# Float32r weight-ring slots at four offsets to a 512-byte line, and the second half of the activations 256 bytes further

## What is computed

```
r, k, v = xr @ w_r, xk @ w_k, xv @ w_v            # 256 x 2048 by 2048 x 2048
y = rwkv7_scan(...)                               # per head, 64 x 64 states
h = layernorm(ALPHA * h + (y_normed * g) @ w_o)
h = layernorm(ALPHA * h + (silu(h @ w_gate) * (h @ w_up)) @ w_down)
k, v, q = h @ kv_w_k, h @ kv_w_v, h @ w_q
h = layernorm(ALPHA * h + attention(q, k, v) @ w_o)
h = layernorm(ALPHA * h + (silu(h @ w_gate) * (h @ w_up)) @ w_down)
```

## Time and profile before

| | us |
|---|---|
| median of three executions | 2487.11 |
| span of the profiled execution, first to last instruction | 2481.7 |
| TensorE busy (matmul) | 2444.9, 99% |
| TensorE weight loads | 2003.2, 81% |
| VectorE busy | 1410.0, 57% |
| ScalarE busy | 1074.4, 43% |
| 16 DMA engines, q1 and q0 | 54.1% and 2.6% |

### The profile page before, as it was taken

How to read it: one execution, slowest core, us unless ns; L and a number is a source line. 1 busy time by engine, 2 the same in 40 slices (tenths; PEclk the granted TensorE clock), 3 DMA queues, 4 the chain that set the end, 5 groups by cost and what they waited for, 6 DMA issues and landing times.

```text
span 2481.7 us, 39434 instructions
## 1 busy us (share of the span) xinstructions
PE 2444.9 (99%) x15550; PEld 2003.2 (81%) x15550; DVE 1410.0 (57%) x1743; ACT 1074.4 (43%) x1347; POOL 126.0 (5%) x166
## 2 busy tenths in 40 slices
PE   8999999999999999999999999999999999999997
PEld 5888788877888888888887788888788888888886
DVE  6688566676744454454446544666745445454445
ACT  4454355444444444443334344453544444443332
POOL 1000235420000000000000000000000000000000
PEclk9999999999999999999999999999999999999999
DMA  7556411255666666665665565445566666666564
GB/s 233 179 195 205 136 42 38 66 208 188 196 192 188 186 193 186 188 188 193 193 195 198 195 193 188 143 167 190 170 187 192 188 186 193 186 194 221 189 194 143
DMA packets 225435, 440.87 MB, mean 178 GB/s; under 512 B 13472, under 2 KB 23744, under 8 KB 224224
## 3 DMA queue, kind: packets, MB, share of 16 engines
q1 hardware_dynamic: 221760, 417.38, 54.1%
q0 software_dynamic: 3552, 21.73, 2.6%
HBM read 436.96 MB, written 2.10 MB: 177 GB/s over the span
## 4 chain that ended last, share of the span: by engine, by line
PE 94%; DVE 3%; ACT 1%; issue 1%; DMA 1%; POOL 0%; DVEq 0%; ACTq 0%; SPq 0%; POOLq 0%
PE ps L595 25%; PE ps L597 25%; PE ps L596 25%; PE ps L892 3%; PE ps L1075 1%; PE ps L775 1%; PE ps L785 1%; PE ps L1103 1%; PE ps L622 1%; PE ps L624 1%; PE ps L623 1%; PE ps L882 1%; PE ps L836 1%; DVE wlo L1684 1%; PE ps L740 1%
## 5 line engine op out<-in xcount | busy, mean ns | idle before, releaser
L1246 ACT CAST whi<-raw 128x1024 fp32r<-128x1024 f32 x735 | 772.5, 1052 | 1145.9 <-PE ps L597 1080.1
L1684 DVE TENSOR_TENSOR wlo<-raw,whi 128x1024 fp32r<-128x1024 f32 x549 | 670.1, 1225 | 622.2 <-ACT whi L1246 620.3
L595 PE MATMUL ps<-whi,ahi 128*128 128x512 f32 x2172 | 851.5, 392 | 2.8 <-DVE wlo L1684 2.8
L597 PE MATMUL ps<-whi,alo 128*128 128x512 f32 x2172 | 845.6, 389 | 0.0
L596 PE MATMUL ps<-wlo,ahi 128*128 128x512 f32 x2172 | 845.1, 389 | 0.0
L595 PEld LDWEIGHTS ps<-whi,ahi 128*128 128x128 f32 x2172 | 407.8, 188 | 87.6 <-DVE wlo L1684 3.6
L597 PEld LDWEIGHTS ps<-whi,alo 128*128 128x128 f32 x2172 | 407.7, 188 | 85.5
L596 PEld LDWEIGHTS ps<-wlo,ahi 128*128 128x128 f32 x2172 | 407.9, 188 | 84.4 <-issue 1.0
L2015 DVE TENSOR_TENSOR wlo<-raw,whi 128x1024 fp32r<-128x1024 f32 x193 | 236.2, 1225 | 249.4 <-ACT whi L1246 247.4
L595 PE MATMUL ps<-whi,hThi 128*128 128x512 f32 x656 | 255.4, 389 | 0.0
L597 PE MATMUL ps<-whi,hTlo 128*128 128x512 f32 x656 | 255.2, 389 | 0.0
(11 more groups left out here) (317 smaller groups left out, 1933.8 us busy)
## 6 DMA issues: line engine op xcount, KB each, us to landing
raw<-w_up SPq DMA_DIRECT2D x176, 512.0 KB, 3.6
raw<-w_down SPq DMA_DIRECT2D x176, 512.0 KB, 4.0
raw<-w_gate SPq DMA_DIRECT2D x170, 512.0 KB, 3.6
raw<-w_k SPq DMA_DIRECT2D x32, 512.0 KB, 3.8
raw<-w_r SPq DMA_DIRECT2D x32, 512.0 KB, 4.4
raw<-w_v SPq DMA_DIRECT2D x32, 512.0 KB, 3.7
raw<-w_o SPq DMA_DIRECT2D x32, 512.0 KB, 4.8
raw<-kv_v SPq DMA_DIRECT2D x32, 512.0 KB, 3.7
```

The lines of the kernel that those rows point to most:

```text
L595: mm(o, hi[:, k, tok], whi[:, s, k2, :], start=(k == 0), stop=False)
L597: last = mm(o, lo[:, k, tok], whi[:, s, k2, :], start=False, stop=(k == kt - 1))
L1246: nc.scalar.copy(whi[:, s], src).then_inc(hi_done, 1)
L1684: V.tensor_tensor(wlo[:, s], src, whi[:, s].bitcast(F32), ALU.subtract).then_inc(split_done, 1)
```

## The change

Only addresses change. No instruction is added, removed or reordered, and no size of an operand changes. The rings `whi` and `wlo` are each one flat tensor that is 128 bytes longer, and slot n is cut from it at n x 4096 bytes plus a skew: 0, 32, 64, 128 bytes in `whi_ring`, 0, 16, 96, 128 bytes in `wlo_ring` (words times four). `alo` lies 256 bytes further behind `ahi`. `pad_ring` shrinks from 176 to 48 words, `pad_act` (64 words) puts `ahi` back onto a multiple of 512, and `pad_big` goes.

```diff
+SKEW_HI = (0, 8, 16, 32)
+SKEW_LO = (0, 4, 24, 32)
+SKEW_ACT = 64
...
-        pad_ring = sb("pad_ring", [P, 176])
+        pad_ring = sb("pad_ring", [P, 48])
         raw = sb("raw", [P, RING, KC, NB])
         with ExitStack() as early:
             rec2 = sb("rec2", [P, 8192], stack=early)
-        whi = sb("whi", [P, RING, KC, NB], F32R)
-        wlo = sb("wlo", [P, RING, KC, NB], F32R)
+        whi_ring = sb("whi_ring", [P, RING * KC * NB + SKEW_HI[-1]], F32R)
+        wlo_ring = sb("wlo_ring", [P, RING * KC * NB + SKEW_LO[-1]], F32R)
+        pad_act = sb("pad_act", [P, 64])
         with ExitStack() as early:
-            a2t = sb("a2t", [P, 8192], stack=early)
+            a2t = sb("a2t", [P, 8192 + SKEW_ACT], stack=early)
         ahi = sb("ahi", [P, KT, T], F32R)
+        pad_alo = sb("pad_alo", [P, SKEW_ACT])
         alo = sb("alo", [P, KT, T], F32R)
...
-        pad_big = sb("pad_big", [P, 32])
...
+        whi = [carve(whi_ring, n * KC * NB + SKEW_HI[n], KC, NB) for n in range(RING)]
+        wlo = [carve(wlo_ring, n * KC * NB + SKEW_LO[n], KC, NB) for n in range(RING)]
...
-        hF = carve(a2t, KT * T, KT, T)
+        hF = carve(a2t, KT * T + SKEW_ACT, KT, T)
...
-                        mm(o, hi[:, k, tok], whi[:, s, k2, :], start=(k == 0), stop=False)
-                        mm(o, hi[:, k, tok], wlo[:, s, k2, :], start=False, stop=False)
-                        last = mm(o, lo[:, k, tok], whi[:, s, k2, :], start=False, stop=(k == kt - 1))
+                        mm(o, hi[:, k, tok], whi[s][:, k2, :], start=(k == 0), stop=False)
+                        mm(o, hi[:, k, tok], wlo[s][:, k2, :], start=False, stop=False)
+                        last = mm(o, lo[:, k, tok], whi[s][:, k2, :], start=False, stop=(k == kt - 1))
```

More of the change, by code:

```diff
@@ L616, in last_job @@
                         s = (ch + (CF if kt == FT else 0)) % RING
-                        wh, wl = (held_hi[ch - per + kept], held_lo[ch - per + kept]) if ch < per - RING else (whi[:, s], wlo[:, s])
+                        wh, wl = (held_hi[ch - per + kept], held_lo[ch - per + kept]) if ch < per - RING else (whi[s], wlo[s])
                         if t == 0:
@@ L1042, in z_chunk @@
                         o, tok, s = ps[:, 2 * b + t, :], slice(t * P, (t + 1) * P), e % RING
-                        mm(o, ahi[:, k, tok], whi[:, s, k2, :], start=(b == 1 and k == 0), stop=False)
-                        mm(o, ahi[:, k, tok], wlo[:, s, k2, :], start=False, stop=False)
-                        last = mm(o, alo[:, k, tok], whi[:, s, k2, :], start=False, stop=(k == KT - 1))
+                        mm(o, ahi[:, k, tok], whi[s][:, k2, :], start=(b == 1 and k == 0), stop=False)
+                        mm(o, ahi[:, k, tok], wlo[s][:, k2, :], start=False, stop=False)
+                        last = mm(o, alo[:, k, tok], whi[s][:, k2, :], start=False, stop=(k == KT - 1))
                 last.then_inc(chunk_used, 1)
@@ L1186, in out_chunk @@
                         o, tok, s = ps[:, 2 * b + t, :], slice(t * P, (t + 1) * P), e % RING
-                        mm(o, ahi[:, k, tok], whi[:, s, k2, :], start=(k == 0), stop=False)
-                        mm(o, ahi[:, k, tok], wlo[:, s, k2, :], start=False, stop=False)
-                        last = mm(o, alo[:, k, tok], whi[:, s, k2, :], start=False, stop=(k == KT - 1))
+                        mm(o, ahi[:, k, tok], whi[s][:, k2, :], start=(k == 0), stop=False)
+                        mm(o, ahi[:, k, tok], wlo[s][:, k2, :], start=False, stop=False)
+                        last = mm(o, alo[:, k, tok], whi[s][:, k2, :], start=False, stop=(k == KT - 1))
                 last.then_inc(chunk_used, 1)
@@ L1245, in split_hi @@
                         act.wait_ge(chunk_used, c + (ch - RING + 1))
-                    nc.scalar.copy(whi[:, s], src).then_inc(hi_done, 1)
+                    nc.scalar.copy(whi[s], src).then_inc(hi_done, 1)
             act.wait_ge(rows_made, 2)
@@ L1525, in norm_affine @@
                 act.wait_ge(chunk_used, c0 + PLAIN - RING + 1)
-                nc.scalar.copy(whi[:, PLAIN], raw[:, PLAIN]).then_inc(hi_done, 1)
+                nc.scalar.copy(whi[PLAIN], raw[:, PLAIN]).then_inc(hi_done, 1)
                 affine(1)
@@ L1536, in held_out @@
                         act.wait_ge(chunk_used, ch - 2 * RING + 1)
-                    nc.scalar.copy(whi[:, s] if late else held_hi[ch - CHUNKS + 2 * RING], raw[:, s]).then_inc(hi_done, 1)
+                    nc.scalar.copy(whi[s] if late else held_hi[ch - CHUNKS + 2 * RING], raw[:, s]).then_inc(hi_done, 1)
             def ffn(layer):
@@ L1683, in split_lo @@
                     src = land[:, LANDED[c + ch]] if isinstance(c, int) and c + ch in LANDED else raw[:, s]
-                    V.tensor_tensor(wlo[:, s], src, whi[:, s].bitcast(F32), ALU.subtract).then_inc(split_done, 1)
+                    V.tensor_tensor(wlo[s], src, whi[s].bitcast(F32), ALU.subtract).then_inc(split_done, 1)
             then(V.memset(xT[:, :, 0:1], 0.0))
@@ L2012, in residual @@
                         e = ch - CHUNKS + 2 * RING
-                        wh, wl = (held_hi[e], held_lo[e]) if 0 <= e < RING else (whi[:, s], wlo[:, s])
+                        wh, wl = (held_hi[e], held_lo[e]) if 0 <= e < RING else (whi[s], wlo[s])
                         dve.wait_ge(hi_done, ch + 1)
```

## The result

The changed kernel takes 2526.14 us (median of four executions, 2524.05 to 2530.14), the kernel before on the same chip 2486.87 (2484.1 to 2488.41). The ratio is 1.016, 95% interval 1.0146 to 1.0174: 39.3 us slower, where 22 us faster was forecast. This is rival A's figure (33 to 39 us), 0.1 us above the top of the range.

A forecast was written before the change was run, and what follows sets the result against it. The prediction took TensorE's matmul stream, 99% busy, as the bound. Its only nonzero term, 22.5 us gained on the step, took the span from 2481.7 to 2459.2 us, so a median of 2464 us, range 2424 to 2526.

The forecast's parts named there:

- rival A: Four slot offsets upset the regular step every 12 matmuls: 33 us slower (2520 us), at most 39 (2526); chance 0.31.
- What bounds the kernel: TensorE is busy 99% of the span and nothing feeds it late; only the matmul stream's own rate counts.
- the count of 9012: 512-column float32r matmuls in the kernel; at 226.7 ns each they fill 2043 us, 82% of the span.
- 9.0 us per nanosecond: Worth of one nanosecond on the step between matmul starts: 9.0 us, 0.36% of the time.
- Instructions, copies, DMA at 0: No instruction changes; ScalarE's copy, VectorE's subtraction and the DMA are covered by idle time: 0 us each.
- The start of an operand matters: Whether operand offsets to a 512-byte line alter TensorE's step; the trace, with one alignment only, could neither confirm nor refute it.
- rows 6: Trace rows behind an interruption: nine uneven steps in 2.08 us, 231 ns each, the shortest 0.22 us.
- I take a gain ... If half of the changed pairs reach it: Half of the changed pairs step 6.7 ns shorter: mean step down 2.5 ns, a gain of 22.5 us.
- the changed pairs: Moving operand against next stationary tile: 3 in 4 of 9012 pairs, about 6760, get new offset differences; bounds -96 to +39 us.
- The lower bound, the plain step of 216: Step of plain float32 matmuls of 256 columns, 10.7 ns below 226.7; reached by every pair it would return 96 us.
- point from which it decides: The slower rival wins once a change of offset upsets the step and no offset wins back over 4 ns.
- Range: Over all cases 2424 us, taking in about half of the large gain, to 2526 us, the slower rival's full price.

The follow-up runs named there:

- offsets_alone: TensorE alone, no kernel: 52 series of 512-column float32r matmuls at set operand offsets; the change's pattern stepped at 231.0 ns, good series settled at 226.7.
- uniform_32: Against the kernel before: all eight slots of both rings at 32 bytes, activations on a 512-byte line; 2541.27 us, ratio 1.0223.
- all_32: Against the kernel before: both rings at 32 bytes and ahi, alo, hThi, hTlo at 32 bytes as well; 2486.78 us against 2485.49, ratio 1.0006.
- offsets_pairs: TensorE alone, no kernel: more matmul series varying offsets, stationary columns and plain float32; moving offsets of 16 to 224 bytes stepped at 231 to 235 ns.
- by_256: The change's form with every skew a multiple of 256 bytes, against the kernel before; 2485.89 us, ratio 1.0003.

## Why the prediction was wrong

- *What bounds the kernel, the count of 9012 and 9.0 us per nanosecond*: right. The loss is in TensorE's stream, and 4.4 ns x 9012 gives the 39.3 us.
- *Instructions, copies, DMA at 0*: right. 1049 and 1224 ns, q1 at 53.5%, the ring waits at 2.4 us. That the other engines do not disturb TensorE's reads is shown by offsets_alone.
- *The start of an operand matters*: right, as rows 6 suggested, and through the pairs of moving and stationary operand as the part on the change set them out. The Trainium skill's page "TensorE: Matmul & The Clock Gate", Part 2, step on LDWEIGHTS, would have had no effect at all here. uniform_32 and all_32 differ only in where the stationary tiles lie against the moving ones, as far as these matmuls go, and by 54 us. So the step that the prediction drew from the page's "doesn't steal", 226.7 ns wherever the operands lie, does not hold, and the measurement decides. Whether the two reads take bandwidth from one another is not shown: shorter weight loads did not shorten the step.
- *"I take a gain ... If half of the changed pairs reach it"*: this is the step that failed. The one term of the sum, the changed pairs, was put at -22.5 us and measured +39.3: the mean step went from 226.7 to 231.0 ns, where 224.2 was forecast. The 0.22 us of rows 6 was one member of an uneven run whose mean was 231, so taking it as a value that a pair could hold was a pick and no bound. It was also misread: the rows give starts to 10 ns, and in the trace's nanoseconds that step is 224, 2.7 ns below 226.7 and not 6.7; no step between matmuls of lines 595 to 597 in the kernel before is shorter. None of the 505 layouts settles below 226.67.
- *The lower bound, the plain step of 216*: reached by none of them either. It is the step of one pass over 256 columns; a pass of plain float32 over 512 columns steps at 429 ns (offsets_pairs). The prediction set it beside the page's 215.8 ns for 512 columns; that the two agree is no test of the page's figure at 512 columns.
- *Rival A* had the size (33 to 39 us for 231 ns; measured 39.3) but not the reason. It blamed the change of offset every 12 matmuls. Slots that differ by 256 bytes cost nothing (by_256), slots that are all alike at 32 bytes cost most (uniform_32). Its "point from which it decides" was wrong. That its number came out is luck: the mean over many layouts, 231.9, happens to lie close to the 231 of the uneven run in rows 6.
- *Range*: its top, 2526, was rival A's full price with nothing beyond it. That bound came from the mean of one uneven run, while single differences hold 233.3 ns (uniform_32, +54.8 us), which the trace of the kernel before could not show.

## What to carry to other kernels

Where TensorE's float32r matmuls follow one another without a gap, look at the start-to-start step and at the offsets of both operands modulo 256 bytes: keep the moving and the stationary operand at the same one, a multiple of 32 bytes. That was worth 12.9 us here where only the down projections had it wrong, and 54.8 where all were 32 bytes apart; which multiple of 32 it is made no difference in the series and kernels above, and a pad ahead of one tensor can shift everything behind it out of step. When a quantity in the trace is uneven, price a disturbance by its mean, not by its best member, and don't take a difference of 7 ns from starts that are given to 10.

## What the runs showed of the hardware that was not expected

- The step of 512-column float32r matmuls tends to settle on a ladder of 6.67 ns per cycle of a pattern: 226.67, 228.89, 231.11, 233.33 ns for patterns of three (314 of 505 series), and 246.67 for the two slowest. Why the ladder exists, and where the 10.7 ns over the plain step come from, no run settles; fewer stationary columns did not lower the step below 226.7.
- One layout can hold two steps: a difference of 64 bytes stepped at 229.2 and 233.4 ns in two runs of TensorE alone; the kernel with it came out at the lower one (+18.1 us).
- A plain float32 matmul is two passes: 40 of them left 80 records and took 34.50 us, 0.86 us each (last rows of offsets_pairs). The 216 ns that the prediction used as its yardstick are the step of one pass over 256 columns.
- At 256 columns the order turns round. The series of 90 float32r matmuls at equal offsets starts 10.79 us before the next, at 32 bytes of difference, and that one 10.61 before the third, at 128: 119.9 and 117.9 ns a step.

```profile
701.45 10.96 PE L232 MATMUL ps<-mov,sta 128*128 128x256 f32 x90
712.24 10.77 PE L225 MATMUL ps<-mov,sta 128*128 128x256 f32 x90
722.85 10.83 PE L232 MATMUL ps<-mov,sta 128*128 128x256 f32 x90
```
